# Norm weights moved from x to the split of gate and up; the first products start at single weight tiles

## What is computed

```python
def rms_norm(x, g):
    y = xf * lax.rsqrt(jnp.mean(xf * xf, axis=-1, keepdims=True) + NORM_EPS)
    return y * g
def swiglu(x, w_gate, w_up, w_down):
    return (silu(x @ w_gate) * (x @ w_up)) @ w_down
h = h + 0.5 * swiglu(rms_norm(h, ln_ffn1[layer]), ffn1_w_gate[layer], ffn1_w_up[layer], ffn1_w_down[layer])
```

## Time and profile before

| | |
|---|---|
| median of 3 runs | 936.85 us |
| profiled execution, its own time | 937.48 us |
| its span | 935.6 us |
| TensorE busy | 923.6 us, 99% |
| VectorE busy | 558.5 us, 60% |
| ScalarE busy | 459.6 us, 49% |
| GpSimd busy | 83.6 us, 9% |
| mean granted TensorE clock | 0.998 |
| DMA | 195.47 MB, mean 209 GB/s |

### The profile page before, as it was taken

One profiled execution on the slowest core, in us unless ns is written; L12 is line 12 of the kernel. 1 busy time (PEld: TensorE's weight loads), 2 busy tenths in 40 slices (PEclk: granted clock), 3 DMA queues, 4 the chain that ended last, 5 costly groups with the idle time before them and its releaser, 6 DMA issues.

```text
span 935.6 us, 11558 instructions
## 1 busy us (share of the span) xinstructions
PE 923.6 (99%) x4322; PEld 758.3 (81%) x4322; DVE 558.5 (60%) x545; ACT 459.6 (49%) x581; POOL 83.6 (9%) x168
## 2 busy tenths in 40 slices
PE   8999999999999999999999999999999999999996
PEld 7878888888877888888888888888876788888885
DVE  5566663554586766665466666654568766666542
ACT  6354643455685544544443454534448654444431
POOL 1510000024311100000004000000030010000000
PEclk9999999999999999999999999999999999999999
DMA  9798876555522677886565778874643368887621
GB/s 317 193 313 259 292 249 234 180 180 180 202 92 90 191 232 251 250 283 231 180 207 164 226 230 249 302 261 158 216 176 99 97 193 250 246 244 291 226 77 45
DMA packets 155707, 195.47 MB, mean 209 GB/s; under 512 B 13448, under 2 KB 127136, under 8 KB 155664
## 3 DMA queue, kind: packets, MB, share of 16 engines
q1 hardware_dynamic: 155328, 194.55, 63.5%
q0 software_dynamic: 320, 0.34, 0.5%
q10 hardware_dynamic: 16, 0.00, 0.0%
HBM read 182.27 MB, written 12.58 MB: 208 GB/s over the span
## 4 chain that ended last, share of the span: by engine, by line
PE 89%; DVE 4%; DMA 3%; ACT 2%; SPq 1%; POOL 0%; issue 0%; POOLq 0%; DVEq 0%; ACTq 0%
PE bank L434 54%; PE bank L471 19%; PE bank L475 10%; PE bank L491 3%; DVE w_lo L1565 2%; DMA h_bounce<-silu 2%; PE bank L622 1%; DMA xn<-h_bounce 1%; PE bank L675 1%; PE bank L597 1%; DMA raw<-in_ffn_w_up 1%; SPq L892 1%; PE bank L615 0%; ACT w_hi L1216 0%; DVE xn L1790 0%
## 5 line engine op out<-in xcount | busy, mean ns | idle before, releaser
L1565 DVE TENSOR_TENSOR w_lo<-raw,w_hi 128x2048 fp32r<-128x2048 f32 x154 | 351.6, 2293 | 192.3 <-ACT w_hi L1216 192.2
L1216 ACT ACTIVATE w_hi<-raw 128x2048 fp32r<-128x2048 f32 x154 | 294.8, 1919 | 188.9 <-PE bank L475 98.2
L434 PE MATMUL bank<-w_hi,xT_hi 128*128 128x512 f32 x832 | 326.2, 392 | 1.3 <-DVE w_lo L1838 0.8
L434 PE MATMUL bank<-w_hi,xT_lo 128*128 128x512 f32 x832 | 324.0, 389 | 0.0
L434 PE MATMUL bank<-w_lo,xT_hi 128*128 128x512 f32 x832 | 323.9, 389 | 0.0
L434 PEld LDWEIGHTS bank<-w_hi,xT_hi 128*128 128x128 f32 x832 | 156.2, 188 | 35.8 <-issue 1.5
L434 PEld LDWEIGHTS bank<-w_hi,xT_lo 128*128 128x128 f32 x832 | 156.2, 188 | 32.6
L434 PEld LDWEIGHTS bank<-w_lo,xT_hi 128*128 128x128 f32 x832 | 156.3, 188 | 31.5
L471 PE MATMUL bank<-w_hi,hT_hi 128*128 128x512 f32 x348 | 135.7, 390 | 0.4 <-DVE h L1620 0.4
L471 PE MATMUL bank<-w_lo,hT_hi 128*128 128x512 f32 x348 | 135.4, 389 | 0.0
L475 PE MATMUL bank<-w_hi,hT_lo 128*128 128x512 f32 x348 | 107.1, 389 | 0.0
(11 more groups left out here) (160 smaller groups left out, 572.9 us busy)
## 6 DMA issues: line engine op xcount, KB each, us to landing
raw<-in_ffn_w_down SPq DMA_DIRECT2D x88, 512.0 KB, 4.9
raw<-in_ffn_w_gate SPq DMA_DIRECT2D x86, 512.0 KB, 4.6
raw<-in_ffn_w_up SPq DMA_DIRECT2D x86, 512.0 KB, 6.0
raw<-in_a_w_qkv SPq DMA_DIRECT2D x24, 512.0 KB, 4.7
h_bounce<-silu SPq DMA_DIRECT2D x40, 256.0 KB, 5.5
xn<-h_bounce SPq DMA_DIRECT2D x160, 64.0 KB, 3.4
raw<-in_a_w_o SPq DMA_DIRECT2D x8, 512.0 KB, 3.7
raw<-in_b_w_q SPq DMA_DIRECT2D x8, 512.0 KB, 5.6
```

What stands on the lines that cost most here:

```text
L434: mm = nc.tensor.matmul(bank[b][:, :], xs[:, kt, own(pos)], ws[:, slot(u), cols], start=(kt == 0 and i == 0), stop=(kt == KT - 1 and i == 2))
L1216: nc.scalar.activation(w_parts(u)[0], raw[:, slot(u), :], ACT.Copy).then_inc(s_hi, 1)
L1565: nc.vector.tensor_tensor(lo, raw[:, slot(u), :], hi.bitcast(F32), ALU.subtract).then_inc(s_lo, 1)
```

## The change

The norm weights are no longer multiplied into x. In units 0 to 21 of the first feed-forward each of the four tiles is scaled by the norm weights of its row block, a per-partition scalar of `first`: on ScalarE w_hi = raw x g, on VectorE w_lo = raw x g - w_hi. One ScalarE and one VectorE instruction per unit become four each; all other units stay as they were. xT_hi and xT_lo of the first norm are made straight from the PSUM banks. In units 0 and 1 every tile has its own signal, and TensorE starts with tile 0. The transposes of position 1 now stand behind the first six products, and the cover transposes are 12 instead of 18 and 2.

```diff
+        def gains_of(u):
+
+            if u < GU_UNITS:
+                return [first[:, 4 * (u % 2) + k:4 * (u % 2) + k + 1] for k in range(4)]
+            return []
...
+                    if pos == 0 and part is not None:
+                        if k == 3:
+                            unit_ready(u)
+                        else:
+                            pe.wait_ge(s_part_lo, 3 * u + k + 1)
...
+                    part_pass(0, 0, 0)
+                    first_transposes(1)
+                    part_pass(0, 1, 0)
+                    part_pass(0, 0, 1)
+                    part_pass(0, 1, 1)
+                    part_pass(1, 0, 0)
+                    part_pass(1, 1, 0)
+                    part_pass(1, 0, 1)
+                    part_pass(1, 1, 1)
...
+            first_transposes(0)
+            warm(12)
...
-                nc.scalar.activation(w_parts(u)[0], raw[:, slot(u), :], ACT.Copy).then_inc(s_hi, 1)
+                for k, gain in enumerate(gains_of(u)):
+                    last = nc.scalar.activation(tile_of(w_hi, u, k), tile_of(raw, u, k), ACT.Copy, scale=gain)
+                if not gains_of(u):
+                    last = nc.scalar.activation(w_parts(u)[0], raw[:, slot(u), :], ACT.Copy)
+                last.then_inc(s_hi, 1)
...
             first_hi(0, 0)
+            act.wait_ge(s_first, 1)
+            split_part(0, 0)
             first_hi(0, 1)
-            split_part(0, 0)
+            split_part(0, 1)
             first_hi(1, 0)
             first_hi(1, 1)
-            split_part(0, 1)
             split_part(1, 0)
             split_part(1, 1)
...
-                nc.vector.tensor_tensor(lo, raw[:, slot(u), :], hi.bitcast(F32), ALU.subtract).then_inc(s_lo, 1)
+                for k, gain in enumerate(gains_of(u)):
+                    last = nc.vector.scalar_tensor_tensor(out=tile_of(w_lo, u, k), in0=tile_of(raw, u, k), scalar=gain,
+                                                          in1=tile_of(w_hi, u, k).bitcast(F32), op0=ALU.mult,
+                                                          op1=ALU.subtract)
+                if not gains_of(u):
+                    last = nc.vector.tensor_tensor(lo, raw[:, slot(u), :], hi.bitcast(F32), ALU.subtract)
+                last.then_inc(s_lo, 1)
...
-            first_gained(0, 0)
-            first_gained(0, 1)
             first_lo(0, 0)
+            split_part(0, 0)
             first_lo(0, 1)
-            split_part(0, 0)
-            first_gained(1, 0)
-            first_gained(1, 1)
+            split_part(0, 1)
             first_lo(1, 0)
-            split_part(0, 1)
             first_lo(1, 1)
             split_part(1, 0)
             split_part(1, 1)
```

More of the change, by code:

```diff
@@ L238, in trunk @@
         s_first = sem("s_first")
-        s_first_lo = sem("s_first_lo")
         s_vec = [sem(f"s_vec{i}") for i in range(VEC_RING)]
@@ L388, in trunk, with tile_of @@
         TABLES = 5
+        def gains_of(u):
+            if u < GU_UNITS:
+                return [first[:, 4 * (u % 2) + k:4 * (u % 2) + k + 1] for k in range(4)]
+            return []
         def part_of(view, u, i):
             return view[:, u, UNIT // 2 * i:UNIT // 2 * (i + 1)]
+        def tile_of(view, u, k):
+            return view[:, slot(u), BANK * k:BANK * (k + 1)]
         @block.tensor
@@ L421, in columns_pass @@
             def columns_pass(u, half, pos, j, key, turn=None, part=None):
-                if pos == 0 and part == 0:
-                    pe.wait_ge(s_part_lo, u + 1)
-                elif pos == 0:
+                if pos == 0 and part is None:
                     unit_ready(u, turn)
@@ L514, in first_turn, with part_pass @@
                 def first_turn():
[L516 to L521, removed]
+                    def part_pass(u, part, pos):
+                        in_sbuf(pe, ("xT", "ln_ffn1_0", pos, u))
+                        columns_pass(u, u, pos, 0, ("gu", f, 0, 0), part=part)
+                    part_pass(0, 0, 0)
[7 more added lines that the diff above has]
+                    part_pass(1, 1, 1)
                     for u in range(2):
@@ L770, in _, with first_transposes @@
             warm(3)
-            for pos in range(NPOS):
+            def first_transposes(pos):
                 pe.wait_ge(s_x[pos], 16)
@@ L774, in _ @@
                     transposes(tiles(x[:, pos, :], j), b, ("xT", "ln_ffn1_0", pos, j))
-                warm((18, 2)[pos])
+            first_transposes(0)
+            warm(12)
             ffn(0, U_FFN1_0, "ln_ffn1_0", "ln_mix_0")
@@ L1372, in split_part @@
                 act.wait_ge((s_part, s_raw)[i][u], 32)
-                nc.scalar.activation(part_of(w_hi, u, i), part_of(raw, u, i), ACT.Copy
-                                     ).then_inc((s_part_hi, s_hi)[i], 1)
+                for k in (2 * i, 2 * i + 1):
+                    nc.scalar.activation(tile_of(w_hi, u, k), tile_of(raw, u, k), ACT.Copy, scale=gains_of(u)[k]
+                                         ).then_inc(s_hi if k == 3 else s_part_hi, 1)
             def first_hi(pos, j):
[L1378 to L1381, removed]
+                hi_part(xT_hi[:, 4 * j:4 * j + 4, own(pos)], x_banks("ln_ffn1_0", pos)[j], ("xT", "ln_ffn1_0", pos, j))
             first_hi(0, 0)
+            act.wait_ge(s_first, 1)
+            split_part(0, 0)
             first_hi(0, 1)
-            split_part(0, 0)
+            split_part(0, 1)
             first_hi(1, 0)
             first_hi(1, 1)
-            split_part(0, 1)
             split_part(1, 0)
@@ L1815, in next_phase @@
                 gained(name, 1, ("wo", layer))
[L1818 to L1825, removed]
-            def first_lo(pos, j):
[L1829 to L1833, removed]
-            def split_part(u, i):
-                dve.wait_ge((s_part_hi, s_hi)[i], u + 1)
-                nc.vector.tensor_tensor(part_of(w_lo, u, i), part_of(raw, u, i), part_of(w_hi, u, i).bitcast(F32),
-                                        ALU.subtract).then_inc((s_part_lo, s_lo)[i], 1)
+            def first_lo(pos, j):
+                tiles_of = slice(4 * j, 4 * j + 4)
+                lo_part(xT_lo[:, tiles_of, own(pos)], xT_hi[:, tiles_of, own(pos)], x_banks("ln_ffn1_0", pos)[j])
+            def split_part(u, i):
+                for k in (2 * i, 2 * i + 1):
+                    if k == 3:
+                        dve.wait_ge(s_hi, u + 1)
+                    else:
+                        dve.wait_ge(s_part_hi, 3 * u + k + 1)
+                    nc.vector.scalar_tensor_tensor(out=tile_of(w_lo, u, k), in0=tile_of(raw, u, k),
+                                                   scalar=gains_of(u)[k], in1=tile_of(w_hi, u, k).bitcast(F32),
+                                                   op0=ALU.mult, op1=ALU.subtract
+                                                   ).then_inc(s_lo if k == 3 else s_part_lo, 1)
             dve.wait_ge(s_filled, filled["first",])
```

## The result

The kernel after takes 940.32 us (median of 5 runs, 938.80 to 943.28), the kernel before beside it 937.37 (936.85 to 938.98): 1.0028 times before, 95% interval 1.0015 to 1.0042, so 0.15% to 0.42% slower. Timed once more with other kernels it was 1.0033 times before (1.0023 to 1.0042). The forecast was 939.9 us; the difference of the medians is +2.95 us where +3.1 were forecast. The profiled execution took 938.80 us, the lowest of the five, 1.32 above the profiled one of before (937.48).

A forecast was written before the change was run, and what follows sets the result against it. TensorE, busy 99% of the span, was taken as the bound, nearly without reserve where chains through h enter it. Terms 1.6 + 0.6 + 0.9 = 3.1 us on a 936.85 us median gave 939.9; range 936.7 to 942.6.

The forecast's parts named there:

- The head, -0.65: Start of the kernel up to unit 2: TensorE starts unit 2 at about 21.45 instead of 22.12 us, gaining 0.65.
- The rule that the halves' wait turns into a wait at unit 2: Head: TensorE's wait at the halves of the first weights is replaced by 0.8 us of waiting for unit 2.
- The price of a unit, +0.47 and +0.44: Splits of 22 units: four scaled pieces cost ScalarE 0.47 and VectorE 0.44 us more, adding to 0.91 on a chain.
- How much of the late write survives, 0.7 of 1.7: First write of h, 33.74 us: issued 1.7 us late by VectorE's dearer splits; 0.7 taken to survive SyncE's queue to unit 11.
- the start of this row would not move by more than 0.1: VectorE's row of splits of units 3 to 6, from 22.89 us: its start shifts by at most 0.1 us.
- the small loads stay put: GpSimd's small transfers, filling the DMA engines near microsecond 35, do not move, so a later write of h meets them less.
- Unit 11, +1.6: TensorE's entry into unit 11 at 63.45 us: 0.7 from the late write plus 0.91 from the split; head's gain lost here.
- Unit 14, +0.6: TensorE's product at 82.64 us: a split dearer by 0.91 against 0.33 us of reserve adds 0.6.
- the h of turn 1 is as late as TensorE: Unit 14: turn 1's h hangs on unit 11's split, as late as TensorE, so only the dearer split counts there.
- The first down product, +0.9: At 132.15 us: unit 21's split and the read of h queued behind it add 0.91 us again.
- The rival that the gain of the head is carried: Earlier split of unit 0 brings all loads sooner; waits at 63.45 and 132.15 us vanish: -2.2 us, 934.6 us; chance 10%.
- The rival by which the covers hold: Splits: pieces cost half, a pair 0.46 us, and the late write is mostly absorbed: +1.3 us, 938.1 us; chance 25%.

The follow-up runs named there:

- second trace of after: The kernel after, unchanged, run once more beside the other experiments: median 941.36 us, 1.0033 times before; its profiled execution took 940.24 us.
- the head alone: The kernel after with only units 0 and 1 scaled by the norm weights, units 2 to 21 split unscaled in one pass: 938.96 us, 1.0003 times before.
- early-write kernel: The kernel after with the third product of h, its silu and its transpose moved ahead of unit 6's split: 940.54 us, 1.0017 times before.
- small loads out of the way: The kernel after with GpSimd's loads of positions, lambdas and biases held until unit 11 has landed: 942.88 us, 1.0055 times before.
- the other order of loads and unscaled units: Head of after, or single-tile starts with x scaled; later units unscaled, loads of units 8 and 9 before the first write of h: 935.51 and 935.28 us.
- the unscaled pieces above: Units 0 and 1 in four unscaled pieces, in the kernel with single-tile starts, x scaled as before, loads 8 and 9 first: 935.28 us, 0.9972 times before.
- the loads of units 8 and 9 first: SyncE issues these loads ahead of the first write and read of h: on the kernel after 937.57 us, on the kernel before 936.89 and 936.64.

## Why the prediction came out

*Direction and size* were right: +2.95 us where +3.1 was forecast. The mechanism was right up to unit 11: dearer splits behind a late h. Behind it the terms were not, and that the total came so close is luck. By how much TensorE is later than in before at four places:

| | unit 2 | unit 11 | unit 14 | first down |
|---|---|---|---|---|
| forecast | -0.67 | +1.6 | +2.2 | +3.1 |
| trace of after | +0.21 | +1.83 | +1.68 | +1.15 |
| second trace of after | +0.11 | +2.35 | +2.22 | +2.74 |

*The head, -0.65.* Wrong, but without effect on the sum, which counted it as lost at unit 11. The first product came at 8.79 (forecast 8.3), unit 2 at 22.33 (21.45). About half of these 0.88 us is the second half of unit 0, which landed at 9.99 and not at 9.55; this varies, 6.3 to 7.4 us from issue to landing over all traces, 6.3 to 6.8 with the head of before. The other half is ScalarE's piece, step 0.61 instead of 0.57: six of them stand in front of the first square, four more in unit 2. The rule that the halves' wait turns into a wait at unit 2 held, with 1.05 us.

*The price of a unit, +0.47 and +0.44.* VectorE right to 0.01 us, ScalarE 0.63. Both together are +1.07, and TensorE's waits between 54 and 66 us (1.91 and 2.35 us in the two traces of the kernel after) are about two of them.

*How much of the late write survives, 0.7 of 1.7.* The write was 2.7 us late, because VectorE's row began 0.95 us later (23.84 against 22.89, behind ScalarE's two dearer units) and took 11.39 us instead of 9.60, 1.79 more (forecast 1.76). The step that failed is that the start of this row would not move by more than 0.1. The second read was issued 0.48 us early in the profiled execution and 1.25 late in the second one (50.77 and 52.50 against 51.25), and its h reached ScalarE 1.12 and 1.61 us late. So the term was too small, and its cause is only in part known: the head alone has 1.27 us there without scaled pieces behind it, and in the early-write kernel an earlier write did not bring the second read forward. With the small loads out of the way this h is at ScalarE at 53.36 us instead of 56.09, so their meeting with the writes is a part of it. It was also argued that the small loads stay put, but they wait for unit 7's load, and moved with it (first issue 32.49 against 31.41).

*Unit 11, +1.6.* In the trace the wait was before unit 10, 1.91 us, and unit 11 followed without one, some 1.8 us late. Sized about right, one unit off: the prediction took unit 11 as the place without reserve, and unit 10, ready at 60.09 for 60.23 in before, had as little.

*Unit 14, +0.6.* Wrong in both traces of the kernel after: no wait. It was argued that the h of turn 1 is as late as TensorE. It was not: its write was issued at 66.13 and 67.20 against 65.93, 0.20 and 1.27 us late, while TensorE was 1.8 and 2.4 late and so had gained reserve. That this place can still be hit the small loads showed with 4.0 us.

*The first down product, +0.9.* Wrong in the first trace: no wait, where before had 0.52, so it gave back 0.5; in the second 0.65, +0.1. The split of unit 21 was later, but the read behind it, issued from 123.43 on instead of 121.36, let ScalarE start at 131.29 instead of 130.14, 1.15 us later and no more than TensorE was.

The sum by the traces is +1.15 and +2.74 us, where the medians give +2.95 and +3.1. Both traces are of the lowest execution of their group. What the others add was not traced and stays open. The granted clocks on record give a hint: of the 91 executions of before beside the experiments, the eight with a mean clock of 0.996 took 939.98 to 944.43 us, where the median of the rest is 938.2. One stretch at half clock as shown above would lower the mean by about 0.002 (an estimate from 3.4 us at 0.50 in 940). That the kernel after has more such stretches is not shown. The rival that the gain of the head is carried fell for this change; the head's gain is carried in part with the other order of loads and unscaled units. The rival by which the covers hold had the overheads of the Trainium skill ("Perfetto Trace Analysis", "Optimizing Scalar/DVE Operations", about 93 ns per ScalarE and 60 ns per VectorE instruction on SBUF): three more instructions cost 0.63 and 0.45 us here, 210 and 150 ns each, so the measurement decides against these figures for passes with a per-partition scalar. For passes without one this case agrees with them: the unscaled pieces above cost 0.26 and 0.20 us more than a whole pass, about 87 and 67 ns for each added instruction. So more than half of the price came with the scaled form of the instructions, and less than half from cutting the pass in four.

## What to carry to other kernels

Work folded into passes that "have room" is paid for where a pass is the last link before the busy engine; find that place by its start times, not by the engine's share. If a queue issues in a fixed order, look first for items whose own condition has long been met: moving two loads ahead of a late write was worth as much as the whole loss, and let a gain through that had been lost behind them. A gain at the head counts only when every later place without reserve moves as well. Follow a delay to the engine that uses the data: a read that was issued early landed late. And compare a repaired kernel with the old one repaired in the same way, or a gain of the repair hides a loss of the change.

## What the hardware showed that I had not expected

A write of 256 KB landed in 2.22 us with nothing in flight before it (and in 2.3 ahead of most small loads), in 5.2 to 6.9 us beside GpSimd's ten small loads in the other twelve traces, and the write of turn 1 in 11.52 us when these met it together with weight loads, against 7.1 to 7.6 us without them.

Four waits of TensorE, 2.20 to 4.00 us long, were each followed by three to four microseconds at a granted clock of 0.50, which cost 1.5 to 1.7 us more.

The executions of one kernel lie 1.2 to 3.1 us apart with the loads of units 8 and 9 first (935.00 to 936.16, 936.72 to 939.79), and 2.7 to 7.8 us in the others (before: 936.60 to 944.43), but for one group of five executions of before, 2.1 us. The groups hold 5 to 35 executions, so this is a rough measure; as far as it goes, a wait on a DMA chain goes with spread as well as time.
